# Gate and up projections of a float32 FFN as seven-product blocks of chunk pairs, and half of the down projection in chunk order

## The reference

```
def swiglu(x, w_gate, w_up, w_down):
    return (jax.nn.silu(x @ w_gate) * (x @ w_up)) @ w_down
...
        h = rmsnorm(x, g_ffn1_pre[i])
        x = x + 0.5 * rmsnorm(swiglu(h, w1_gate[i], w1_up[i], w1_down[i]), g_ffn1_post[i])
...
    x = x + swiglu_ffn(rms_norm(x, norm_ffn), w_gate_up, w_down)
```

## Time and profile before

| | us |
|---|---|
| median of three runs | 3401.55 |
| lowest and highest run | 3396.91, 3402.91 |
| profiled execution, span from first to last instruction | 3402.3 |
| PE busy in it | 3319.4 |
| POOL busy | 2409.4 |
| DVE busy | 1688.1 |
| ACT busy | 715.6 |

### The profile page before, as it was taken

How to read it: one execution, slowest core, us unless ns; L and a number is a source line. 1 busy time by engine, 2 the same in 40 slices (tenths; PEclk the granted TensorE clock), 3 DMA queues, 4 the chain that set the end, 5 groups by cost and what they waited for, 6 DMA issues and landing times.

```text
span 3402.3 us, 42134 instructions
## 1 busy us (share of the span) xinstructions
PE 3319.4 (98%) x15389; PEld 2625.4 (77%) x15389; DVE 1688.1 (50%) x1899; ACT 715.6 (21%) x1447; POOL 2409.4 (71%) x1115
## 2 busy tenths in 40 slices
PE   8999999999999999999999999998999999999998
PEld 7888775788887888877578887765788887778886
DVE  5444344555657545244465475679444314464521
ACT  3111125311114111023421112325311101241100
POOL 8888762588886888875178888662488787648875
PEclk9999999999999999999999999999999999999999
DMA  3223220222332223322022233210122233212232
GB/s 133 98 94 108 93 87 32 74 93 99 108 120 72 99 93 102 105 83 92 19 87 94 97 115 106 105 66 28 62 93 98 99 105 107 75 57 99 96 102 93
DMA packets 84367, 305.15 MB, mean 90 GB/s; under 512 B 9360, under 2 KB 9616, under 8 KB 83984
## 3 DMA queue, kind: packets, MB, share of 16 engines
q1 hardware_dynamic: 80928, 292.59, 25.4%
q10 hardware_dynamic: 3312, 10.86, 0.9%
HBM read 299.22 MB, written 4.19 MB: 89 GB/s over the span
## 4 chain that ended last, share of the span: by engine, by line
PE 88%; DVE 5%; issue 3%; ACT 3%; DMA 0%; DVEq 0%; ACTq 0%
PE psC L605 12%; PE psC L607 12%; PE psC L606 12%; PE psA L605 8%; PE psA L607 8%; PE psA L606 8%; PE psB L606 4%; PE psB L607 4%; PE psB L605 4%; PE psC L1080 2%; PE psC L1081 2%; PE psC L1082 1%; DVE stat L1825 1%; DVE X L1614 1%; ACT HH L1278 1%
## 5 line engine op out<-in xcount | busy, mean ns | idle before, releaser
L529 POOL TENSOR_TENSOR WH<-raw,scalars 128x1024 fp32r<-128x1024 f32 (+1 forms) x554 | 1047.8, 1891 | 923.2 <-DMA raw<-in_w 853.0
L531 POOL TENSOR_TENSOR WL<-raw,WH 128x1024 fp32r<-128x1024 f32 (+1 forms) x554 | 1359.4, 2454 | 43.5
L605 PE MATMUL psA<-HH,WH 128*128 128x512 f32 x1136 | 454.7, 400 | 1.2 <-DVE Y L1682 1.2
L607 PE MATMUL psA<-HL,WH 128*128 128x512 f32 x1136 | 442.9, 390 | 0.0
L606 PE MATMUL psA<-HH,WL 128*128 128x512 f32 x1136 | 442.8, 390 | 0.0
L605 PE MATMUL psC<-HIDH,WH 128*128 128x512 f32 x1056 | 416.1, 394 | 0.0
L607 PE MATMUL psC<-HIDL,WH 128*128 128x512 f32 x1056 | 414.0, 392 | 0.0
L606 PE MATMUL psC<-HIDH,WL 128*128 128x512 f32 x1056 | 409.8, 388 | 0.0
L1687 DVE TENSOR_TENSOR HIDL<-Y,HIDH 128x512 f32 (+1 forms) x132 | 255.1, 1932 | 125.7 <-ACT HIDH L1327 125.7
L605 PE MATMUL psC<-HH,WH 128*128 128x512 f32 x704 | 275.9, 392 | 0.0
L606 PE MATMUL psC<-HH,WL 128*128 128x512 f32 x704 | 274.3, 390 | 0.0
(11 more groups left out here) (375 smaller groups left out, 4803.9 us busy)
## 6 DMA issues: line engine op xcount, KB each, us to landing
raw<-in_w SPq DMA_DIRECT2D x554, 512.0 KB, 3.3
X<-in_x ACTq DMA_DIRECT2D x4, 512.0 KB, 9.3
NRAW<-in_mem ACTq DMA_DIRECT2D x2, 1024.0 KB, 5.6
out<-Y SPq DMA_DIRECT2D x8, 256.0 KB, 2.1
POSI<-in_pos ACTq DMA_DIRECT2D x4, 256.0 KB, 2.6
PRAW<-in_p ACTq DMA_DIRECT2D x2, 512.0 KB, 4.0
table_F<-newF ACTq DMA_DIRECT2D x2, 512.0 KB, 2.7
table_I<-newI ACTq DMA_DIRECT2D x2, 512.0 KB, 3.8
```

The costliest lines, as they stand in the source:

```text
L529: pool.tensor_tensor(WH[j][:, 0:w], raw[j][:, 0:w], zero[:, 0:1].broadcast_to([P, w]), ALU.subtract).then_inc(w_hi, 1)
L531: pool.tensor_tensor(WL[j][:, 0:w], raw[j][:, 0:w], WH[j][:, 0:w], ALU.subtract).then_inc(w_split, 1)
L605: pe.matmul(out, WH[slot][:, w], hi[:, t], start=start and t == 0, stop=False)
L607: mm = pe.matmul(out, WH[slot][:, w], lo[:, t], start=False, stop=stop and t == tiles - 1)
```

## The change

Chunks 0 to 3 of gate and up stay as they are (8 pieces). Chunks 4 to 21 go as nine pairs, chunk m with chunk m + 9. In a pair, weights and activations are cut in two by chunk, by features (512 and 512) and by tokens (256 and 256), and the four block products become seven (Strassen's scheme in Winograd's form): seven products of 24 matmuls of 256 columns each. Sums of activations (TF, with high and low parts TH and TL) are made once per FFN by DVE and ACT at its start, out of BF, the gain times X. Sums of weights are made for every pair: SP loads A, C, B, A again and D (from a second input, `ws`), two DMAs that POOL issues add to what lies in a slot (D to C, C to the second A), and POOL adds twice. The high parts WH of the seven weights are then copies by ACT (`high`), the low parts subtractions by DVE (`low`). ACT copies finished partial results from bank to bank (the seeds), and DVE combines and scales them. Each quarter of a pair's hidden values lands in HID; HIDH and HIDL are made from HID after the pairs, the first six chunks during the last pair. Of the down projection, outputs 0 to 3 are now computed together, chunk after chunk, in psA and psB (12 pieces); outputs 4 to 7 as before in psC. Some host code lays out the weights accordingly, and ACT's loop over the two layers is written out twice.

```diff
+        def product(i, slots, out, start, hi, lo):
+            pe.wait_ge(part_lo, n.full(part_lo))
+            slot = slots[i]
+            for half in range(2):
+                o = out[:, tokens_of(half)]
+                for k in range(HALF_K):
+                    w = slice((half * HALF_K + k) * P, (half * HALF_K + k + 1) * P)
+                    pe.matmul(o, WH[slot][:, w], hi[:, k], start=start and half == 0 and k == 0, stop=False, skip_group_check=True)
...
+            mm.then_inc(part_used, 1)
+        def pair(p, slots):
...
+            product(0, slots, b0, True, HH[:, near, t0], HL[:, near, t0])
+            product(1, slots, b1, True, TH[0], TL[0])
+            pe.wait_ge(seeded, n.full(seeded))
+            product(2, slots, b2, False, TH[1], TL[1])
+            product(3, slots, b0, False, HH[:, far, t0], HL[:, far, t0])
+            pe.wait_ge(seeded, n.full(seeded, 2))
+            product(4, slots, b2, False, TH[2], TL[2])
+            product(5, slots, b3, False, HH[:, far, t1], HL[:, far, t1])
+            pe.wait_ge(left_read, n.full(left_read))
+            product(6, slots, b2, False, TH[3], TL[3])
...
+        def sums(slots, first):
+            v = n.room(pair_index)
+            pool.wait_ge(c_in, n.full(c_in, 16))
+            add_to(slots[1], v, 2, cd_in)
+            if not first:
+                pool.wait_ge(part_used, n.full(part_used, 3))
+            pool.wait_ge(a_in, n.full(a_in, 16))
+            pool.wait_ge(cd_in, n.full(cd_in, 16))
+            pool.tensor_tensor(raw[slots[2]][:], raw[slots[1]][:], raw[slots[0]][:], ALU.add).then_inc(sum_ready, 1)
+            pool.wait_ge(sum_ready, n.full(sum_ready))
+            if not first:
+                pool.wait_ge(part_used, n.full(part_used, 3))
...
+            pool.wait_ge(b_in, n.full(b_in, 16))
+            pool.tensor_tensor(raw[slots[5]][:], raw[slots[2]][:], raw[slots[3]][:], ALU.add).then_inc(sum_ready, 1)
...
+            pool.wait_ge(a2_in, n.full(a2_in, 16))
+            add_to(slots[4], v, 1, ac_in)
...
+            with n.loop(PAIRS - 1):
...
+                sp.wait_ge(part_used, n.full(part_used))
+                part(slots[0], v, 0, a_in)
+                sp.wait_ge(part_used, n.full(part_used))
+                part(slots[1], v, 1, c_in)
+                sp.wait_ge(part_used, n.full(part_used, 2))
+                part(slots[3], v, 3, b_in)
+                sp.wait_ge(part_used, n.full(part_used))
+                part(slots[4], v, 0, a2_in)
+                sp.wait_ge(part_used, n.full(part_used, 2))
+                part(slots[6], v, 2, d_in)
...
+            for k in range(KD):
+                act.activation(BF[:, k], X[:, k], ACT.Copy, scale=gain(k)).then_inc(bf_ready, 1)
+            silu(0)
+            silu(1)
+            for i in (0, 2, 1, 3):
+                act.wait_ge(tf_ready, n.full(tf_ready))
+                act.activation(TH[i][:], TF[i][:], ACT.Copy).then_inc(th_ready, 1)
...
+            def low(i):
+                dve.wait_ge(part_hi, n.full(part_hi))
+                if i in (0, 2):
+                    dve.wait_ge(sum_ready, n.full(sum_ready))
+                dve.tensor_tensor(WL[slots[i]][:], raw[slots[i]][:], WH[slots[i]][:], ALU.subtract).then_inc(part_lo, 1)
...
+            dve.wait_ge(bf_ready, n.full(bf_ready, KD))
+            for i, a, b, sign in ((0, BF[:, near, t0], BF[:, near, t1], None), (2, BF[:, far, t1], BF[:, near, t1], None),
+                                  (1, TF[2][:], BF[:, near, t0], -1.0), (3, TF[1][:], BF[:, far, t0], -1.0)):
...
+            hidden(0)
+            hidden(1)
...
+            for i in (0, 2, 1, 3):
+                dve.wait_ge(th_ready, n.full(th_ready))
+                dve.tensor_tensor(TL[i][:], TF[i][:], TH[i][:], ALU.subtract).then_inc(tl_ready, 1)
+            hidden(2)
+            low(0)
+            low(1)
+            hidden(3)
...
+            for ks in EARLY_K:
+                pe.wait_ge(w_split, n.full(w_split))
+                slot = next_slot()
+                for j, k in enumerate(ks):
+                    pe.wait_ge(hid_ready, hid + k + 1)
+                    for m in range(EARLY_M):
...
+                        pe.matmul(down_bank(m), WH[slot][:, w], HIDH[:, k], start=k == 0, stop=False)
...
-                act.activation(SQ[:, m % 2], PC[:, m % 2], ACT.Square).then_inc(ysq_ready, 1)
-                act.activation(Y[:, m], PC[:, m % 2], ACT.Copy).then_inc(out_free, 1)
+                act.activation(SQ[:, m % 2], bank, ACT.Square).then_inc(ysq_ready, 1)
+                act.activation(Y[:, m], bank, ACT.Copy).then_inc(out_free, 1)
```

More of the change, by code:

```diff
@@ L1 @@
 from contextlib import ExitStack, contextmanager
+from dataclasses import dataclass
 import numpy as np
@@ L548, in border, with add_to @@
             split(RING + 1, TILES)
-        def down():
-            with n.loop(2):
-                for q in range(12):
-                    ring(1, DOWN[q % 3])
-        def ffn():
-            border()
-            rounds(36)
-            ring(2)
-            down()
-        def plain_ffn():
-            n.full(hl_ready, KD)
-            rounds(UP_PIECES)
-            down()
+        def add_to(slot, v, j, s):
+            pool.dma_start(raw[slot][:], A["ws"][bass.ds((v - 1) * 4 + j, 1)].rearrange("a p n -> p (a n)"), accum_op=ALU.add).then_inc(s, 16)
@@ new lines, in ffn @@
+        def ffn(normed=True):
+            slots = part_slots(normed)
+            if normed:
+                ring(RING)
+                pool.wait_ge(hl_ready, n.full(hl_ready, 6))
+                n.full(hl_ready, 2)
+                split(SPARE, TILES)
+                split(SPARE + 1, TILES)
+                split(0, TILES)
+                split(SPARE, TILES)
+                pool.wait_ge(piece_used, n.full(piece_used, 4))
+                n.full(piece_used, FFN_PIECES - 4)
+            else:
+                n.full(hl_ready, KD)
+                ring(RING + 2)
+                split(SPARE, TILES)
+                split(SPARE + 1, TILES)
+                pool.wait_ge(piece_used, n.full(piece_used, 5))
+                n.full(piece_used, FFN_PIECES - 5)
+            sums(slots, True)
+            with n.loop(PAIRS - 1):
+                sums(slots, False)
+            n.full(part_used, PRODUCTS)
+            nonlocal_turn(0)
+            for ks in EARLY_K:
+                ring(1, len(ks) * EARLY_M)
+            for q in range(DOWN_PIECES - EARLY_PIECES):
+                ring(1, DOWN[q % 3])
@@ L703, in ffn @@
                     whole(up_bank(m))
-            def gate_and_up(m):
                 pe.wait_ge(gu_free, n.room(gu_free))
-                whole(gate_bank(m))
-                whole(up_bank(m))
-            with n.loop((KF - 4) // 6):
-                for m in range(3, 9):
-                    gate_and_up(m)
-            gate_and_up(KF - 1)
-            pe.wait_ge(gu_free, n.room(gu_free, 2))
-            n.room(gu_free)
+                whole(gate_bank(3), SPARE)
+                whole(up_bank(3), SPARE + 1)
@@ new lines, in ffn @@
+            taken = 0
+            pe.wait_ge(gu_free, n.room(gu_free, 2))
+            pe.wait_ge(tl_ready, n.full(tl_ready, 4))
+            pair(0, slots)
+            pe.wait_ge(gu_free, n.room(gu_free))
+            pair(1, slots)
+            with n.loop((PAIRS - 3) // 2):
+                for p in range(2):
+                    pe.wait_ge(quad_done, n.full(quad_done, 4))
+                    pair(p, slots)
+            pe.wait_ge(quad_done, n.full(quad_done, 4))
+            pair(0, slots)
@@ L716, in ffn @@
             hid = n.now(hid_ready)
             n.full(hid_ready, KF)
-            with n.loop(2):
-                for m in range(4):
-                    output_room(normed)
-                    for q, tiles in enumerate(DOWN):
-                        pe.wait_ge(hid_ready, hid + 8 * q + tiles)
-                        pe.wait_ge(w_split, n.full(w_split))
-                        piece(next_slot(), PC[:, m % 2], HIDH[:, 8 * q:], HIDL[:, 8 * q:], tiles, q == 0, q == 2)
+            pe.wait_ge(quad_done, n.full(quad_done, 4))
@@ new lines, in ffn @@
+            pe.wait_ge(quad_done, n.full(quad_done, 4))
+            for m in range(KD):
+                room = n.room(out_free) if normed else n.full(x_ready) - 2
+                if m < EARLY_M:
+                    continue
+                if m >= EARLY_M + 2:
+                    pe.wait_ge(out_free if normed else x_ready, room)
+                for q, tiles in enumerate(DOWN):
+                    pe.wait_ge(w_split, n.full(w_split))
+                    piece(next_slot(), down_bank(m), HIDH[:, 8 * q:], HIDL[:, 8 * q:], tiles, q == 0, q == 2)
@@ L1340, in ffn @@
                 return
-            outputs(3, (tabM,) if layer is None else (newF, newI))
+            outputs(3, (tabM,) if layer is None else (newF, newI), down_bank)
         def squares_room(m):
@@ L1500, in _ @@
         input_norm(lambda k: w_col(W_FIRST + k))
-        with n.loop(DEPTH) as layer:
```

(13 more changed lines are left out.)

320 lines of the change are left out of this document (269 added, 51 removed).

## The result

The changed kernel takes 3552.98 us (median of 4 runs, 3539.7 to 3558.5), the kernel before 3402.23 beside it: the ratio is 1.0439, 95% interval 1.0416 to 1.0463. It is slower by 4.4%. The profiled execution has a span of 3552.9 us, 150.6 more than the one before.

What follows compares the result with a forecast made beforehand. PE, busy 98% of the span, was taken as the bound. Terms -105 + 38 + 12 + 6 + 48 + 36 + 2 + 12 = +49 on 3402.3 gave about 3450 us, range 3360 to 3560.

Steps and rivals of the forecast that it cites:

- the slot loop: Pair loop: product 1 ends, C loads, D is added, POOL sums, low(0) follows; period 20.8 for 19.8, +48 us.
- point of decision: Pair loop: an adding DMA landing in under 5.2 us costs nothing; a later one lets POOL's second sum delay low(0).
- L: Pair loop: time POOL's DMA needs to add D to C, taken as 5.3 us, between 3.3 and 9.3.
- the period of 15.5 + L: Pair loop: length of a turn if the first sum comes late and POOL's second sum, 2.4 us, precedes low(0).
- the accumulating DMA is slow: Rival, pair loop: L about 7.8, so +168 in place of +48, total 3570 us; chance 0.15.
- the long stalls at six places: Stalls of 6 to 19 us were to lower PE's granted clock, 2 us each: +12 (4 to 20).
- The saving: Gate/up chunks 4 to 21: 1512 matmuls of 256 columns replace 864 of 512; -105 us over six FFNs.
- The starts: FFN starts: PE waits at chunk 3 and before product 0; +38, +12, and +6 for E and F; +64 with clock.
- The down projection: Output 6 waits for ACT's copy of output 4 behind sines: +36 in B and D, +2 in A and C.
- Nothing on PE: Down projection: the same 528 matmuls in another order were to cost PE no extra time, 0 us.
- The rival of the other sign: FFN starts and pair loop: DVE isn't blocked by POOL; -69 us, total 3381, chance 0.30.
- The quick DMA: Rival, pair loop: L under 5.2, all else as forecast; -48 us, total 3402, chance 0.12.

Runs made afterwards that it cites:

- e1: Changed kernel with the addition of D to C left out, all loads and other work kept: 3438.37 us, ratio 1.0107.
- e2: Changed kernel with the sum A+C+D taking A from its second copy before C is added there, so low(0) need not wait for it: 3490.23 us.
- e5: Changed kernel with DVE reading chunks 0 and 1 out before the T sums, and ACT's silus before the BF copies: 3560.51 us, ratio 1.0448.

## Why the prediction was wrong

**The failed step is the price of the slot loop.** The forecast had found the loop, its members and its point of decision; it put +48 on it and it cost 129: the 48 distances are 2.6 us above PE's 19.97 in the mean, where 1.0 was forecast. Its links were mis-sized; the numbers are those of the turn in FFN B. The load of C is issued at 6.6 and not at 5.7, 0.9 more. It was put at 3.3 us, the median of the kernel before; with the load of A under way beside it (the DMA share of this stage is 0.60, before it was 0.29) it lands after 4.6, and POOL issues the addition after 5.4, 2.1 more. The adding DMA was put at L = 5.3; it lands after 7.15, and from POOL's issue to the sum it is 7.3, 2.0 more. In the other direction, POOL's second sum was given precedence over `low(0)`, 2.4 us, and DVE goes first; `low(0)` and the step to product 0 take 0.4 less. Net: 23.0 in place of 20.8.

The price was also not firm by the prediction's own figures. The first sum ready at 11.5 + L and product 5 ending at 17.0 put the point at L = 5.5 and not at 5.2, so that L = 5.3 would have cost nothing; and the period of 15.5 + L holds 0.5 us that no link of the list has.

Of the rivals, "the accumulating DMA is slow" (L of 7.8, 3570), to which 0.15 was given, is nearest: L is 7.1 to 7.3. That its total is only 17 off is in part luck, as it had POOL's sum ahead of `low(0)`, which did not happen, and the load of C at 3.3.

**The clock belongs to the price of the waits.** Most products 0 waited 1 to 4 us. The forecast gave 12 us of clock to the long stalls at six places and none to the short ones in the loop; those cost about 42 by the clock and 12 at their edges, on 75 of waits. Run e1 had no such waits in its loop and a clock of 1.00 there. Run e2 had one of 0.8 us in each pair and a clock of 1.00 too, so here it was the long waits that came with the lower clock.

**The saving** was right: -105 forecast from 96 matmuls elsewhere in the trace, -97 measured. By the sustained gaps of the Trainium skill ("TensorE: Matmul & The Clock Gate", section "Back-to-back issue gap") the stage would have become slower by 35 per FFN with no stall at all (an estimate from that page); e1 shows 16 less. The measurement decides against these two figures of the page for this kernel.

**The starts** came out as 51 us against 64 with the clock, and the mechanism was the one named: 33.8 at chunk 3 and 7.9 in front of product 0 (C, E and F); 9 have no wait. That reordering moves this wait but does not remove it was seen only in e5.

**The down projection:** the stalls in B and D were 20.4 and 20.1 against 18 forecast, and A and C had none (124.0 and 123.7, the same as E), against 2. What the forecast missed is a term that it put at nothing, 18 us in all: the same 528 matmuls take 0.2333 us from start to start instead of 0.2289 (14 us), and the first three of a stage 0.7 us more (4 us). "Nothing on PE" rested on the count alone. The slower pace is shown, its cause is not; stages outside the FFNs have it too.

**The rival of the other sign** (DVE not held by POOL, 3381) was half true: DVE was not held, and it did not matter, as its own condition L below 6.7 failed. The quick DMA fell with it, since L is above 7. The two pages of the Trainium skill ("DMA: Bandwidth & Descriptors", section "Anatomy of one DMA — SWDGE (gpsimd) path", and "Collectives: The Full Stack", section "The bandwidth ceiling: the fold count and why AG ≠ RS ≠ AR") gave an estimate of 4.4; the trace does not agree, as the addition in the loop lands after 7.1 and the quickest of all 108 after 5.2.

## What to carry to other kernels

When a change halves work on the bounding engine, list every loop that closes through a buffer (who frees it, what refills it, what is done to it) and add up each link's duration with its issue and its wait; a link that no trace shows should be measured by itself before anything is built on it. Take a transfer's duration from a stretch with the traffic that the new kernel will have, one kind of transfer at a time, and follow the loop to every consumer: in e2 the next wait was 0.8 us behind the one that was cut. And price a gap on TensorE by its length: the waits of the changed kernel, most of them 1 to 4 us, cost about 0.7 of their length on top, mostly in matmuls at half clock behind them, those of 0.8 us in e2 about 0.3 us each and no clock. Before a slower matmul is put down to one edit, look whether stages that the edit leaves alone have slowed as well.

## What was not expected of the hardware

An adding DMA of 512 KB takes 7.1 us to land (median of the 48 that add D to C in the loop, 5.5 to 8.6) or 5.5 (the other one of each pair), against 3.6 for the plain loads of `in_w` in the same kernel. When DVE's `low(0)` and POOL's second sum both become free to start on the end of POOL's first sum, DVE goes first in all 48 turns (888.05 against 888.27 in the one shown), and the second sum is stretched (3.23 for 2.4 us). And matmuls of 512 columns run 2% slower (250 against 255 in 58 us) in stages whose activations lie in a region of SBUF that the change shifted, written out or looped, while chunks 1 and 2 of FFN E, which read everything from its old place, keep 0.2269 us in written-out code; the cause stays open.
